# Moving operand sums from VectorE to ScalarE and GpSimd DMAs, and another order of 64 modulation products

## The reference

```
for i in range(DEPTH):                       # DEPTH = 2
    sh1, s1, g1, sh2, s2, g2 = split(silu(c) @ ada_w[i] + ada_b[i], 6)   # also for the context, with c_ctx
    x = layernorm(ALPHA * x + g1 * mixer(x * (1 + s1) + sh1)) * ln1_g + ln1_b
    x = layernorm(ALPHA * x + g2 * (square(relu((x * (1 + s2) + sh2) @ w1)) @ w2)) * ln2_g + ln2_b
    # layer 0 does the same for the context tokens
```

## Time and profile before

| | |
|---|---|
| median of three runs | 1970.19 us |
| the profiled execution | 1970.03 us, of which the profile's span is 1968.2 us |
| PE busy | 1950.2 us (99%) |
| DVE busy | 1312.8 us (67%) |
| ACT busy | 643.3 us (33%) |
| POOL busy | 385.8 us (20%) |
| mean granted TensorE clock | 0.997 of full |

### The profile page before, as it was taken

How to read it: one execution, slowest core, us unless ns; L and a number is a source line. 1 busy time by engine, 2 the same in 40 slices (tenths; PEclk the granted TensorE clock), 3 DMA queues, 4 the chain that set the end, 5 groups by cost and what they waited for, 6 DMA issues and landing times.

```text
span 1968.2 us, 25026 instructions
## 1 busy us (share of the span) xinstructions
PE 1950.2 (99%) x9525; PEld 1670.1 (85%) x9525; DVE 1312.8 (67%) x1892; ACT 643.3 (33%) x894; POOL 385.8 (20%) x360
## 2 busy tenths in 40 slices
PE   9999999999899999999999999999999999999998
PEld 6889889889789988888888888888888888888887
DVE  4756678688687777767774553553554477777778
ACT  3423222245223322232524223223323344444443
POOL 0300311322221222212350020020020026200004
PEclk9999999999999999999999999999999999999999
DMA  9613333236898999989422131221222125977656
GB/s 338 246 65 76 108 128 129 96 108 158 181 248 219 226 224 241 241 226 245 123 71 65 43 102 65 65 91 54 69 71 81 54 86 172 230 218 194 178 144 149
DMA packets 112737, 286.62 MB, mean 146 GB/s; under 512 B 16368, under 2 KB 29296, under 8 KB 112496
## 3 DMA queue, kind: packets, MB, share of 16 engines
q1 hardware_dynamic: 86400, 223.02, 33.9%
q0 software_dynamic: 24400, 58.21, 17.0%
q10 hardware_dynamic: 1824, 3.85, 0.6%
HBM read 238.34 MB, written 2.12 MB: 122 GB/s over the span
## 4 chain that ended last, share of the span: by engine, by line
PE 89%; issue 3%; DMA 2%; POOL 2%; DVE 2%; ACT 1%; SPq 1%; POOLq 0%; DVEq 0%; ACTq 0%
PE bank L1000 17%; PE bank L1002 16%; PE bank L1001 16%; PE bank L1038 7%; PE bank L1039 7%; PE bank L1040 7%; PE bank L1401 3%; PE bank L1403 2%; PE bank L1404 2%; PE bank L1603 2%; PE bank L1605 2%; PE bank L1606 2%; PE bank L1357 1%; PE bank L1308 1%; DMA wsum<-wsum 1%
## 5 line engine op out<-in xcount | busy, mean ns | idle before, releaser
L2100 DVE TENSOR_TENSOR w_lo<-raw,w_hi 128x1024 fp32r<-128x1024 f32 x132 | 171.3, 1298 | 244.2 <-ACT w_hi L1629 244.1
L1629 ACT ACTIVATE w_hi<-raw 128x1024 fp32r<-128x1024 f32 x132 | 139.4, 1056 | 370.2 <-PE bank L1040 199.1
L1038 PE MATMUL bank<-w_hi,hT_hi 128*128 128x512 f32 x592 | 230.6, 390 | 0.0
L1039 PE MATMUL bank<-w_lo,hT_hi 128*128 128x512 f32 x592 | 230.4, 389 | 0.0
L1040 PE MATMUL bank<-w_hi,hT_lo 128*128 128x512 f32 x592 | 230.3, 389 | 0.0
L1000 PE MATMUL bank<-w_hi,act_hi 128*128 128x512 f32 x504 | 199.3, 395 | 1.8 <-DVE rbuf L2239 1.8
L1002 PE MATMUL bank<-w_hi,act_lo 128*128 128x512 f32 x504 | 197.1, 391 | 0.0
L1001 PE MATMUL bank<-w_lo,act_hi 128*128 128x512 f32 x504 | 197.0, 391 | 0.0
L1000 PE MATMUL bank<-hT_hi,w_hi 128*128 128x384 f32 (+2 forms) x544 | 192.2, 353 | 0.0
L1001 PE MATMUL bank<-hT_lo,w_hi 128*128 128x384 f32 (+2 forms) x544 | 190.8, 351 | 0.0
L1002 PE MATMUL bank<-hT_hi,w_lo 128*128 128x384 f32 (+2 forms) x544 | 190.8, 351 | 0.0
(11 more groups left out here) (389 smaller groups left out, 4336.1 us busy)
## 6 DMA issues: line engine op xcount, KB each, us to landing
raw<-w_units_d SPq DMA_DIRECT2D x242, 512.0 KB, 3.7
wsum<-w_units_d SPq DMA_DIRECT2D x52, 512.0 KB, 5.0
mod<-mod_units_d SPq DMA_DIRECT2D x64, 384.0 KB, 5.6
wsum<-w_units_d POOLq DMA_DIRECT2D x26, 512.0 KB, 7.3
wsum<-wsum POOLq DMA_DIRECT2D x26, 512.0 KB, 6.6
bv<-mod_units_d SPq DMA_DIRECT2D x16, 512.0 KB, 3.5
mod<-mod_units_d SPq DMA_DIRECT2D x14, 512.0 KB, 8.2
res_lat<-rbuf POOLq DMA_DIRECT2D x28, 256.0 KB, 5.2
```

The source lines that it names most:

```text
L1038: nc.tensor.matmul(bank[t][:, :], hT_hi[:, kc, tt], hi[:, c], start=kc == 0, stop=False)
L1039: nc.tensor.matmul(bank[t][:, :], hT_hi[:, kc, tt], lo[:, c], start=False, stop=False)
L1629: nc.scalar.activation(halves_of(phase, k, i)[0], raw[:, s, :], ACT.Copy).then_inc(hi_done, 1)
L2100: tt(lo, raw[:, s, :], f32(hi), ALU.subtract).then_inc(lo_done, 1)
```

## The change

Five things change.

1. The three whole blocks x21, x22, x11 are no longer added up by DVE. ACT copies their high parts (three activations after the block c = 1), and POOL adds the low parts with six accumulating DMAs (`add_operand`, two for each block, 128x2x384 each). DVE waits for all six right after block c = 2 and then makes the first two differences, ahead of the squares of block c = 3.
2. The sum for s4 likewise: two DMAs add the high part and two the low part, in between the DMAs of the first piece's residual. ACT waits for them (`s4_whole`) ahead of the split of T2.
3. The multiplication of the six residual tiles by the gain goes from DVE to POOL (`ln_scale_shift`, twelve 128x512 instructions), ahead of the new DMAs. POOL's sums T1 and T2, which stood at the head, now follow T3 behind the six new DMAs.
4. SP loads T3's base instead of T1's early, T1's after `shifted0`.
5. The last modulation group is spread over the pieces 3, 4 and 5, and the last piece does all eight products of group 6 (2 at each of the places 0 to 3) instead of five.

```
 MOD1_SEQ = [(g, n) for g in range(PIECES_MIXED) for n in range(KC)]
-MOD1_SEQ += [(g, n) for g in range(PIECES_MIXED, PIECES_F) for n in range(KC)]
-MOD1_PLACES = [[1, 1, 2, 2, 2]] * 3 + [[1, 2, 2, 2, 3], [2, 2, 2, 2, 3], [2, 2, 2, 2, 3, 3], [2, 3]]
+for _p, _a, _b in ((3, 0, 2), (4, 2, 5), (5, 5, 8)):
+    MOD1_SEQ += [(_p, n) for n in range(KC)] + [(7, n) for n in range(_a, _b)]
+MOD1_SEQ += [(6, n) for n in range(KC)]
+MOD1_PLACES = [[1, 1, 2, 2, 2]] * 3 + [[1, 2, 2, 2, 3]] + [[1, 2, 2, 3, 3]] * 2 + [[2, 2, 2, 2]]
...
-        SLOT0 = {T1: 1, T2: 2, T3: 0, T4: 1}
+        SLOT0 = {T1: 0, T2: 1, T3: 2, T4: 0}
...
-            load_base0(0, T1)
-            load_base0(0, T2)
             for k in range(RAW):
                 weights(at + k)
+            load_base0(0, T3)
+            load_base0(0, T2)
+            sp.wait_ge(shifted0, 16 * TILES0)
+            load_base0(0, T1)
...
-            sp.wait_ge(shifted0, 16 * TILES0)
-            load_base0(0, T3)
...
+                    if phase == "ffn0a" and c == 1:
+                        for dst, k, t in ((x21, first, t_second), (x22, second, t_second), (x11, first, t_first)):
+                            nc.scalar.activation(dst[:, :, :], hT_hi[:, k, t].bitcast(F32), ACT.Copy).then_inc(x_copied, 1)
+                    if phase == "ffn0a" and c == 2:
+                        operand0_hi(1, x22, s1_hi[:, :, :])
                 if phase == "ffn0a":
+                    operand0_hi(2, x21, OPERANDS0[7][0])
                     split_hi(phase, i, 5, used_unit(phase, i, 3))
-                    operand0_hi(1, x22, s1_hi[:, :, :])
-                    operand0_hi(2, x21, OPERANDS0[7][0])
                     operand0_hi(3, x22, s2_hi[:, :, :])
                     split_hi(phase, i, 6, used_unit(phase, i, 4))
                     split_hi(phase, i, 7, used_unit(phase, i, 5))
-                    operand0_hi(4, x22, s4_hi[:, :, :])
                     block0_hi(0, 0)
+                    act.wait_ge(s4_whole, 64)
+                    nc.scalar.activation(s4_hi[:, :, :], x22[:, :, :], ACT.Copy).then_inc(s_hi0, 1)
                     block0_hi(0, 1)
...
-                        if c == 0:
...
-                            whole_operand(x11, first, t_first)
...
-                        for t in ((0,), (1, 2), (3, 4), (5,))[c]:
-                            tt(res(t), res(t), lnbc0[:, 0, :], ALU.mult).then_inc(res_mul, 1)
+                    if phase == "ffn0a" and c == 2:
+                        for n in range(3):
+                            dve.wait_ge(x_whole[n], 32)
+                        operand0_sum(1, x22, x21, x22)
+                        operand0_sum(2, x21, x11, x21)
...
-                    tt(x22[:, :, :], x22[:, :, :], f32(hT_hi[:, second, t_first]), ALU.add).then_inc(x_whole, 1)
...
-                    tt(x22[:, :, :], x22[:, :, :], f32(hT_lo[:, second, t_first]), ALU.add).then_inc(s_sum0, 1)
...
+            def ln_scale_shift():
+                pool.wait_ge(lnbc_scaled, 1)
+                pool.wait_ge(stage_lo, before("stage", "ln0a") + 2 * KC)
+                for t in range(TILES0):
+                    for h in range(2):
+                        c = slice(h * 512, (h + 1) * 512)
+                        gt(res(t)[:, c], res(t)[:, c], lnbc0[:, 0, c], ALU.mult).then_inc(res_mul, 1)
+                    pool.wait_ge(res_mul, BASE_MUL["ln0a"] + 2 * t + 2)
+                    nc.gpsimd.dma_start(res(t), lnbc0[:, 1, :], accum_op=ALU.add).then_inc(shifted0, 16)
+            def add_operand(dst, src, k, t, whole):
+                for h in range(2):
+                    part = slice(k.start + 2 * h, k.start + 2 * h + 2)
+                    nc.gpsimd.dma_start(dst[:, 2 * h:2 * h + 2, :], src[:, part, t].bitcast(F32), accum_op=ALU.add).then_inc(whole, 16)
...
-            weight_sum0(0, T1)
-            weight_sum0(0, T2)
-            shift_by_dma0()
-            weight_sum0(0, T3)
+            ln_scale_shift()
+            for n, (dst, k, t) in enumerate(((x21, first, t_second), (x22, second, t_second), (x11, first, t_first))):
+                pool.wait_ge(x_copied, n + 1)
+                add_operand(dst, hT_lo, k, t, x_whole[n])
+            for x in (T3, T1, T2):
+                weight_sum0(0, x)
             pool.wait_ge(shifted0, 16 * TILES0)
+            pool.wait_ge(s_lo0, 3)
+            add_operand(x22, hT_hi, second, t_first, s4_whole)
             add0(-1, 0)
+            pool.wait_ge(s4_whole, 32)
+            add_operand(x22, hT_lo, second, t_first, s4_whole)
             add0(-1, 1)
```

More of the change, by code:

```diff
@@ L434, in build @@
         gy_added = [sem(f"gy_added{t}") for t in range(TILES0)]
-        x_whole = sem("x_whole")
+        x_copied = sem("x_copied")
+        x_whole = [sem(f"x_whole{x}") for x in range(3)]
         s_sum0 = sem("s_sum0")
@@ L438, in build @@
         s_lo0 = sem("s_lo0")
+        s4_whole = sem("s4_whole")
         shifted0 = sem("shifted0")
@@ L1409, in rows @@
                     pe.wait_ge(mod_used, len(MOD1_SEQ) if phase == "ffn0z" else MOD1_SEQ.index((p, KC - 1)) + 1)
-                    mod_sums(phase, i, "rows0", 6, [sum1(p), sum1(PIECES_F - 1 if phase == "ffn0z" else p, 1)],
+                    mod_sums(phase, i, "rows0", 6, [macc[:, 0, :], macc[:, 0 if PIECES_MIXED <= p < PIECES_F - 2 else 1, :]],
                              WIDE_M1 // 2)
@@ L2249, in done, with products @@
                     dve.wait_ge(dve_drain, drained(phase, i, f"q{q}.{j}")[1])
-                def products(place, at=None):
-                    here = places[place] if place < len(places) else ()
-                    for n in here if at is None else here[at:at + 1]:
+                def products(place):
+                    for n in places[place]:
                         mod_product(n)
@@ L2342, in ffn0 @@
                         drain0(p, 1, t)
-                        if t < TILES0 - 1:
-                            products(5, t - 2)
                     block0_lo(p + 1, 1)
@@ L2771, in mod_product @@
                 elif g:
-                    dve.wait_ge(pe_step, step_of("ffn0", g - 1 if g <= PIECES_MIXED else g - 2, "rows0"))
+                    dve.wait_ge(pe_step, step_of("ffn0", g - 1 if g < 7 else PIECES_MIXED - 1, "rows0"))
                 unit = mod1[:, n % SLOTS_M1, :]
                 for v in reversed(range(2 if g < PIECES_MIXED else 1)):
-                    acc = sum1(g, v)
+                    acc = macc[:, 1 if g == 7 else v, :]
                     if kc == 0:
@@ L2802, in gate_unit @@
                     .then_inc(gated, 1)
-            def whole_operand(out, k, t):
-                tt(out[:, :, :], f32(hT_hi[:, k, t]), f32(hT_lo[:, k, t]), ALU.add).then_inc(x_whole, 1)
             def operand0_sum(n, out, a, b):
@@ L2856, in ffn @@
                 if phase == "ffn0a":
-                    dve.wait_ge(x_whole, 3)
-                    operand0_sum(1, x22, x21, x22)
+                    operand0_lo(1, x22, s1_lo[:, :, :], s1_hi[:, :, :])
                     split_lo(phase, i, 5)
-                    operand0_sum(2, x21, x11, x21)
-                    operand0_lo(1, x22, s1_lo[:, :, :], s1_hi[:, :, :])
                     operand0_sum(3, x22, x22, x11)
@@ L2873, in ffn @@
                     split_lo(phase, i, 7)
-                    dve.wait_ge(x_whole, 4)
-                    tt(x22[:, :, :], x22[:, :, :], f32(hT_lo[:, second, t_first]), ALU.add).then_inc(s_sum0, 1)
                     block0_lo(0, 0)
@@ L3110, in weight_sum0 @@
                 nc.gpsimd.dma_start(out, other, accum_op=ALU.add).then_inc(t_sum0[x], 16)
-            def shift_by_dma0():
-                for t in range(TILES0):
-                    pool.wait_ge(res_mul, BASE_MUL["ln0a"] + t + 1)
-                    nc.gpsimd.dma_start(res(t), lnbc0[:, 1, :], accum_op=ALU.add).then_inc(shifted0, 16)
+            def add_operand(dst, src, k, t, whole):
+                for h in range(2):
+                    part = slice(k.start + 2 * h, k.start + 2 * h + 2)
+                    nc.gpsimd.dma_start(dst[:, 2 * h:2 * h + 2, :], src[:, part, t].bitcast(F32), accum_op=ALU.add).then_inc(whole, 16)
             def add0(p, half):
```

13 lines of the change are left out of this document (1 added, 12 removed).

## The result

The changed kernel takes 2025.16 us (median of four runs, 2023.84 to 2025.53); the kernel before took 1970.33 us beside it. The ratio is 1.0275, 95% interval 1.0257 to 1.0293. The forecast was 2011 us with a range of 1988 to 2022: the direction is right, the size is not, and the time lies 3 us above the range. The profiled execution took 2024.92 us, 54.9 us more than that of before.

What follows compares the result with a forecast made beforehand. PE bounds the kernel, so only its waits count. Front (31.2 + 1.6 + 8.1 + 1.6 − 8.5 = +34.0 us) and modulation products (+7.2) add 41.2 to 1970.03: 2011 us, 8-in-10 range 1988 to 2022.

Steps and rivals of the forecast that it cites:

- What bounds the kernel: Whole kernel: PE is busy 1950.2 of 1968.2 us, so only its waits, or taking them away, can move the time.
- the 8.5 us: First piece (ffn0a): two PE stalls and slow clock behind them lose 2.0 + 1.6 + 3.4 + 1.5 us, counted as winnable.
- Part 1: First piece: sums and gain multiplications leaving DVE free it of 16 us; ACT's three copies cost nothing, at most 0.3 us.
- Part 2: POOL's queue: operand DMAs start about 489.5 us, go one by one 5.0 us apart, the sixth lands at 519.4 us.
- Rival A: POOL's queue does not hold the operand DMAs apart, or they are short: 1988.5 us; chance 0.14.
- 384 pieces in flight: POOL's DMA queue: 384 pieces fit in flight and 512 do not, so two 256-piece operand DMAs can't overlap.
- Part 3: First down product: PE stops at 498.2 us, resumes at 529.3, a stall of 31.2 us, and 1.6 for the clock.
- Part 4: Ahead of q6: s4_whole comes at 563.5 us, so PE stalls 8.1 us, and 1.6 for the clock.
- Part 5: Modulation products: 6.2 us stall at the last piece's rows step, 1.6 clock, 0.7 load, less 1.3: +7.2 us.
- The clock: PE's granted clock falls to half behind each of three forecast stalls, costing 1.6 us each time.
- Rival B: Transfers as slow as from HBM, or POOL multiplies at 1.89 us: 2016 for one, 2027 for both; chance 0.14.

Runs made afterwards that it cites:

- best: Kernel before, with two DVE instructions moved in the first piece and the modulation products of pieces 4 and 5 placed as in places45: 1968.6 us, ratio 0.9990.
- places45: Kernel before, with only the modulation products of pieces 4 and 5 put at other places: 1968.8 us, ratio 0.9989.
- poolgain: Kernel before, with only the multiplication by the gain moved from DVE to POOL: 1975.1 us, ratio 1.0023.
- dvegain: Changed kernel, with the multiplication by the gain back on DVE: 2024.4 us, ratio 1.0278.
- ring1344: Changed kernel, with descriptor memory (dynamic_dma_scratch_size) raised from 1024 to 1344: 2007.6 us, ratio 1.0192.
- splate: Changed kernel, with SP's loads of the bases of T3 and T2 put behind the six residual transfers: 2022.2 us, ratio 1.0264.
- before_mod: Kernel before, with only the order and places of the 64 modulation products changed: 1975.3 us, ratio 1.0027.
- latewait: Changed kernel, with DVE's wait for the three whole blocks and the first differences moved behind unit 7, ACT's likewise: 2024.6 us, ratio 1.0276.
- xdve: Changed kernel, with x21, x22, x11 added up on DVE again, without ACT's copies and the six operand DMAs: 1996.7 us, ratio 1.0135.
- s4dve: Changed kernel, with the two s4 sums back on DVE and the four s4 DMAs gone: 2010.8 us, ratio 1.0205.

## Why the prediction was wrong

**What bounds the kernel: half right.** PE's waits were the right thing to read, and PE was held at the places named. But the 8.5 us were not to be had: best takes most of both stalls away and gains 2.1 us, of which places45 has 1.9 without touching that piece. PE then waits for a weight sum that lands no earlier, and the clock falls behind that wait.

**Part 1 (DVE freed of 16 us, ACT's copies at nothing): wrong.** That POOL's multiplications hold DVE up was not priced, though the 1885 ns and 1287 ns of the earlier trace rows hinted at it from POOL's side; poolgain shows 14.2 us of it in the kernel before. In the changed kernel ACT's copies (478.81 to 483.04 us without a gap) stand ahead of a ReLU besides, and PE waits 2.4 us for it. Without POOL's multiplications (dvegain) that stall is gone with the copies still there.

**Part 2 (first operand DMA at 489.5): the step that failed.** It says that the first operand DMA starts when only one residual transfer is in flight, and that POOL reaches it at 487.3 us. It was issued at 501.00. The term that failed is the wait in POOL's queue: 2.2 us ahead of the operand DMAs and nothing ahead of the residual transfers, where 5.1 and 5.8 us were measured. Multiplications were right (18.4 us for 18.0). Issues took 0.96 us each, 2.2 us more in all. Then came what was left out: the residual transfers are held apart by the same queue, the third lay behind SP's 1.5 MB, POOL stood 5.8 us for it, and the first operand DMA waited 5.1 us, not 2.2, until none was in flight. 2.2 + 5.8 + 2.9 and 0.6 of small things are the 11.5 us. ring1344 shows that the queue's memory holds the transfers apart, splate that SP's loads made the third one late. That these DMAs go one by one was right: 4.7 us apart, forecast 5.0. Rival A (1988.5) is out for this queue, and even with more of that memory (ring1344) the time stays 19 us above it. The count behind this part, 384 pieces in flight, fails for the residual transfers. By it the fourth would have been issued at 481.7 us beside the third, and the first operand DMA at 495.9 beside the sixth; both waited until nothing was in flight. In dvegain the last three residual transfers were issued within 1.1 us all the same. What the queue counts stays open.

**Part 3: right in its own terms.** From the landing until PE resumes it took 9.1 us, forecast 9.9 (the sum there gives 9.7, so 529.1 and not 529.3). The stall is 38.1 us because PE resumes 11.5 us later (540.85 for 529.3) and stopped 4.4 us later (the new stall, and the clock at half behind it).

**Part 4: right in kind.** s4 whole 47.2 us behind the operands (578.9 less 531.7), forecast 44.1; PE at q6 31.3 us behind its resumption, forecast 30.4. With 4.5 us from s4 to q6 (forecast 4.3) and 9.1 from the landing to PE's resumption (9.9) the stall is 47.2 + 4.5 − 9.1 − 31.3 = 11.3 us, where 44.1 + 4.3 − 9.9 − 30.4 = 8.1 was forecast. What was sized too small are the two weight sums ahead (13.6 us for 12.4) and T2 with the first pair for s4 (15.1 for 12.5).

**Part 5: right.** The stall is 5.9 us for 6.2, the whole part by itself (before_mod) 5.6 us (3.3 to 7.3) for 7.2, and the short waits are gone.

**The clock: mis-sized.** 1.6 us for each stall was read behind waits of 2 to 3 us; behind those of 6 us and more it was 1.7 to 2.9, and a fourth stall brought 1.4.

Sum: PE resumes ahead of q6 at 583.4 where 567.8 was forecast, 15.6 us late: 11.5 from the start of the operand DMAs, 0.9 on the way and 3.2 in the second stall. The error of the whole is 13.7 (54.9 less 41.2), so 1.9 us came back behind it; where is not shown. Rival B gave 2016 to 2027 us, but for reasons that did not come: landings were 4.4 us and POOL multiplied at 1.5.

## What to carry to other kernels

Before work is given to a queue, add up what stands in it already, from the first transfer that it shares resources with, and compare the sum with the work that runs beside it; if the queue is longer, moving the wait about changes nothing (latewait), and only fewer or overlapping transfers do (xdve, s4dve, ring1344). An elementwise operation moved from VectorE to GpSimd is to be priced at what it takes from VectorE as well: here twice what it gave. And a stall that is seen in a profile is worth its length only if what stands behind it (here a weight sum whose load shares full DMA engines) can come earlier too.

## What the runs showed of the hardware

- Descriptor memory sets how many GpSimd DMAs overlap: with 1024 bytes a partition 256-piece DMAs run one at a time, 4.69 us apart; with 1344, in pairs, 3.53 us apart.
- GpSimd multiplications of 128x512 from SBUF beside VectorE hold it up: 128x384 low parts take 1880 ns on average instead of 556, 128x1024 low parts 2340 instead of 1218. A low part that meets a pair of them takes 3.2 us, one that doesn't about 0.55. A VectorE sum that starts first keeps its time (1.75 us), and the multiplication takes 2.35 us for 1.6.
- After a stall of 38 us TensorE resumed at half clock and lost 2.5 us, no more than after one of 6 us (2.9).
